# Eight experts' rows: gathers and scatters as indirect DMAs through DRAM, only expert 0 gathered by products, residual and output by token

## The chip, the core and the metric

The kernel runs on one core of one Trainium2 chip. The metric is the device time of one execution in microseconds (us), the median of three runs. All values are float32. The core's engines are TensorE (PE, its weight loads shown as PEld), VectorE (DVE), ScalarE (ACT), GpSimd (POOL) and SyncE (SP), and 16 DMA engines serve its queues. SP's queue carries the loads of weights here.

## The reference

A block of two layers over 256 tokens of width 1024. Layer 0 (a gated linear recurrence, an RWKV-7 mixer, a dense SwiGLU) and the mixer of layer 1 (mLSTM) are not touched by the change. It touches the last part, the mixture of experts, the residual add behind it and the final norm:

```python
def moe_swiglu(xn, w_router, w1, w3, w2):        # xn = rms_norm(x, norm_ffn), 256 x 1024
    logits = (xt @ w_router).astype(jnp.float32)  # 8 experts
    top_logit, top_idx = lax.top_k(logits, TOP_K) # 2 of them per token
    gates = jax.nn.softmax(top_logit, axis=-1)
    ...
    yb = lax.map(expert_block, (buf.reshape(nblk, EXPERT_BLOCK, D), blk_e))  # silu(x @ w1) * (x @ w3) @ w2, hidden 2816
    y_slot = yb.reshape(P, D)[dest] * sorted_g[:, None].astype(xn.dtype)
    out = jnp.zeros((T, D), xn.dtype).at[sorted_tok].add(y_slot)
```

Then `x + moe_swiglu(...)`, and the final RMS norm with its weight `final_norm` gives the output, 256 x 1024.

## The kernel before

Every engine has a program of its own, written by hand; semaphores order them (`wait_ge` on one, `then_inc` on the other). Activations `x` (the residual) and `xn` are kept transposed, 8 tiles of 128 channels x 256 tokens (`KD` = 8). The layers before the experts end near 552 us.

**Routing.** From the router's logits VectorE computes, for each token (128 tokens on the partitions, `CH` = 2 chunks) and each expert, the slot that the token takes among the expert's 96 (`SLOTS`), in `rt[:, 14:16, :]`. If some expert has more than 96 tokens, `flag` is set and the experts run again for further slots (`PASSES`); each engine loads `flag` and branches at the end. With these inputs the second pass isn't run.

**Gather.** `gather_matrices` writes one-hot matrices `OH` (token x slot, scaled by the token's inverse root mean square), and TensorE's `gather` multiplies the tokens, turned to token-major in `xtok`, with them, in three groups of experts, `GATHERS = ((0, 2), (2, 5), (5, 8))`, into PSUM. ScalarE's `gathered` copies the result with the norm's weight to `xg`, 128 channels x 8 x 96 slots for each expert.

**Stages.** `up(n, g)` is half an expert's first two products: for each of 8 weight tiles of 1408 KB (a ring of `USLOTS` = 9 buffers), 24 matmuls of 352 columns, four side by side in the four column groups. ScalarE's `gate` takes the SiLU of it, VectorE's `hidden` multiplies and turns it into `hidT`, 32 x 32 blocks at a time. `down(n, e, p)` takes a pair of second-product weight tiles of 512 KB each (a ring of `DSLOTS` = 7), three turns of four matmuls of 512 columns; eleven pairs make an expert. Its output lies in PSUM banks 6 and 7, where ScalarE's `expert_out` copies it to `ye` (slots on the partitions).

**Scatter.** `scatter_rows` writes `OHg` (one-hot by slot, scaled by the gate; it lies over `hidT`), `scatter_matrices` transposes it on TensorE to `SG`, and `scatter(n, e, r)` multiplies `ye` with it: four matmuls of 256 columns for each half `r` of the channels. VectorE's `add` adds each half to `x`.

**The order around it**, on TensorE, for an expert e: up(2e+2), down pairs 5 to 10 of e, up(2e+3), down pairs 0 to 4 of e+1, with the scatter of e behind pairs 1 and 2. SP's loads follow the same order in `refills`, one load when a buffer is through, waited for in order:

```python
                    refill_up(n, 2 * e + 1)
                    for p in range(5):
                        refill_down(n, NB * e + p)
                    if e < E - 1:
                        refill_up(n, 2 * e + 2)
                    for p in range(5, NB):
                        refill_down(n, NB * e + p)
```

The tile of down pair p that comes free is refilled with the tile 7 further on, three and a half pairs later. Behind the last expert: the branch on `flag`, ScalarE squares `x` (8 tiles of channels), TensorE's `norm_mean` sums over channels, ScalarE's root, VectorE's reciprocal and `normed` write the output's 8 channel tiles, each stored by SP to `out_T`. POOL has no work after 500 us.

## Time and profile before

| | us |
|---|---|
| median of 3 runs | 1334.25 (1334.09 to 1346.22) |
| the profiled execution | 1339.85 |
| its span, first to last instruction | 1338.1 |
| granted TensorE clock, mean | 0.988 |
| HBM read, written | 344.71 MB, 1.05 MB |

A page of the profile gives each engine's busy time and share of the span, the span in 40 slices, the DMA queues, the chain of work that ended last, and groups of like instructions. A float32 matmul call stands in the trace as two matmul records and two weight load records. Four matmuls that run side by side count once in busy time. The name `W` is one large buffer that holds the weight rings (and `ye`, `rt`), `S` one that holds `xg`, `hidT`, `SG` and `OH`, `ps` is PSUM.

### The profile page before, as it was taken

How to read it: one execution, taken by the hardware profiler on the slowest of the kernel's cores; microseconds unless marked ns; L12 is line 12 of the kernel's file. 1: busy time of each engine (PE TensorE's matmuls, PEld its weight loads, DVE VectorE, ACT ScalarE, POOL GpSimd, SP SyncE). 2: the span in 40 equal slices, each digit the busy share in tenths (PEclk: the TensorE clock that was granted, in tenths of full speed). 3: DMA queues.
4: the chain of work that ended last, by engine and by line, in shares of the span. 5: the costliest groups of instructions: out<-in, count | busy, mean ns of one | idle time of the engine just before them, and what ended most of it. 6: DMA issues, size and time to landing. Idle time of an engine off the chain costs nothing.

```text
span 1338.1 us, 26356 instructions
## 1 busy us (share of the span) xinstructions
PE 1284.5 (96%) x12327; PEld 779.4 (58%) x12327; DVE 279.4 (21%) x605; ACT 180.7 (14%) x378; POOL 15.1 (1%) x14
## 2 busy tenths in 40 slices
PE   6999999999999998999999999999999999999995
PEld 5888888888888886754434434434344344344332
DVE  2657462000002734320000001001001000010012
ACT  3415311000001234310101010000000010100002
POOL 0012000000000000000000000000000000000000
PEclk9999999999999998999999999999999999999998
DMA  9500095454007344387899999999999999999551
GB/s 358 206 1 2 25 341 197 148 184 146 1 0 304 116 188 173 154 347 276 318 383 382 351 408 392 353 380 381 387 391 361 376 377 362 405 391 363 193 208 63
DMA packets 72918, 347.56 MB, mean 260 GB/s; under 512 B 5720, under 2 KB 13272, under 8 KB 56160
## 3 DMA queue, kind: packets, MB, share of 16 engines
q1 hardware_dynamic: 72496, 345.68, 66.9%
q8 instruction: 99, 1.62, 0.5%
q10 hardware_dynamic: 304, 0.10, 0.1%
q14 instruction: 19, 0.16, 0.0%
HBM read 344.71 MB, written 1.05 MB: 258 GB/s over the span
## 4 chain that ended last, share of the span: by engine, by line
PE 91%; DMA 4%; DVE 2%; ACT 1%; issue 1%; DVEq 0%; SPq 0%; ACTq 0%
PE ps L480 91%; DMA W<-in_moe 4%; DMA cf<-in_cf 1%; DVE rs L1347 0%; DVE W L1465 0%; DVE xn L1354 0%; ACT S L1231 0%; ACT S L1136 0%; DVE S L1462 0%; DVE W L1464 0%; ACT W L1290 0%; DVE W L1500 0%; DVE W L1498 0%; ACT L1239 0%; ACT L1136 0%
## 5 line engine op out<-in xcount | busy, mean ns | idle before, releaser
L480 PE MATMUL ps<-W,S 128*32 128x352 f32 (+2 forms) x8384 | 701.1, 491 | 13.7 <-DMA W<-in_moe 11.5
L480 PEld LDWEIGHTS ps<-W,S 128*32 128x32 f32 (+1 forms) x8384 | 280.6, 111 | 424.9 <-issue 377.2
L480 PE MATMUL ps<-xn,W 128*128 128x256 f32 (+1 forms) x1456 | 324.4, 383 | 3.2 <-DVE xn L1354 3.0
L480 PEld LDWEIGHTS ps<-xn,W 128*128 128x128 f32 (+1 forms) x1456 | 277.2, 191 | 46.3 <-issue 7.2
L480 PE MATMUL ps<-S,W 128*128 128x256 f32 (+3 forms) x728 | 161.0, 372 | 2.5 <-ACT W L1290 2.5
L1734 DVE TENSOR_TENSOR S<-S,ps 128x352 f32<-128x352 f32 x48 | 25.0, 521 | 589.8 <-ACT S L1282 586.5
L480 PEld LDWEIGHTS ps<-S,W 128*128 128x128 f32 (+3 forms) x728 | 128.5, 186 | 33.2 <-issue 12.8
L1282 ACT ACTIVATE S<-ps 128x352 f32<-128x352 f32 x48 | 20.5, 462 | 544.6 <-PE ps L480 540.9
L480 PE MATMUL ps<-W 64*64 64x64 f32 (+1 forms) x1296 | 50.5, 224 | 3.2 <-DVE W L1500 1.6
L480 PEld LDWEIGHTS ps<-W 64*64 64x64 f32 (+1 forms) x1296 | 46.7, 137 | 7.8 <-issue 4.1
L1562 DVE TENSOR_TENSOR S<-S,ps 128x256 f32<-128x256 f32 x20 | 8.4, 421 | 194.6 <-ACT S L1184 194.6
L1290 ACT ACTIVATE W<-ps 64x512 f32<-64x512 f32 x32 | 18.9, 591 | 143.4 <-PE ps L480 143.1
L1723 DVE TENSOR_TENSOR x<-x,ps 128x1024 f32<-128x1024 f32 x16 | 19.5, 1221 | 69.7 <-PE ps L480 69.7
L1184 ACT ACTIVATE S<-ps 128x256 f32<-128x256 f32 x20 | 7.7, 383 | 195.6 <-PE ps L480 195.6
L1741 DVE STREAM_TRANSPOSE S<-S 128x352 f32<-128x352 f32 x48 | 26.2, 545 | 15.1 <-PE ps L480 11.4
L480 PE MATMUL ps<-xn,cf 128*128 128x256 f32 x32 | 13.4, 607 | 14.5 <-DMA cf<-in_cf 8.8
L480 PE MATMUL ps<-S,xn 128*128 128x288 f32 (+1 forms) x96 | 23.1, 402 | 1.3 <-DVE S L1692 1.0
L480 PEld LDWEIGHTS ps<-S,xn 128*128 128x128 f32 x96 | 18.5, 204 | 5.6 <-issue 1.1
L480 PEld LDWEIGHTS ps<-xn,cf 128*128 128x128 f32 x32 | 10.1, 324 | 17.3 <-DMA cf<-in_cf 8.8
L1060 ACT ACTIVATE S<-x 128x256 f32<-128x256 f32 x24 | 9.0, 416 | 57.4 <-DVE x L1536 57.4
L1536 DVE TENSOR_TENSOR x<-x,ps 128x256 f32<-128x256 f32 x24 | 9.0, 417 | 24.1 <-PE ps L480 24.0
L1354 DVE SCALAR_TENSOR_TENSOR xn<-x,vec,rs 128x256 f32<-128x256 f32 x32 | 13.0, 479 | 0.1
(232 smaller groups left out, 382.8 us busy)
## 6 DMA issues: line engine op xcount, KB each, us to landing
W<-in_moe SPq DMA_DIRECT2D x128, 1408.0 KB, 8.3
W<-in_moe SPq DMA_DIRECT2D x176, 512.0 KB, 6.3
W<-in_l_ffn_w SPq DMA_DIRECT2D x12, 2048.0 KB, 10.4
W<-in_l_w_in SPq DMA_DIRECT2D x5, 2048.0 KB, 21.1
W<-in_l_ffn_w SPq DMA_DIRECT2D x6, 1536.0 KB, 13.6
W<-in_l_w_out SPq DMA_DIRECT2D x2, 4096.0 KB, 20.4
...
```

Source lines behind the costliest of these rows:

```text
L480: return nc.tensor.matmul(o, l, r, start=start, stop=stop, **kw)
L1060: A_(squares[:, k, :], x[:, k, :], ACT.Square).then_inc(sq_done, 1)
L1184: A_(sil0[:, f % 4, :], ps[:, 4 + f % 4, 0:T], ACT.Silu).then_inc(silu_done, 1)
L1282: A_(sil[:, i % 2, :], ps[:, 2 * t, 0:QN], ACT.Silu).then_inc(m_silu, 1)
L1290: ins = A_(ye[64 * b2:64 * b2 + 64, 512 * i:512 * (i + 1)], ps[64 * i:64 * i + 64, 6 + b2, :], ACT.Copy)
L1354: V.scalar_tensor_tensor(dst[:, k, :], x[:, k, :], col(name, k), rs[:, :], ALU.mult, ALU.mult).then_inc(xn_done, 1)
L1536: V.tensor_tensor(x[:, 2 * d + u, :], x[:, 2 * d + u, :], ps[:, d, u * T:(u + 1) * T], ALU.add).then_inc(res_done, 1)
L1562: V.tensor_tensor(hid0[:, f % 4, :], sil0[:, f % 4, :], ps[:, 4 + f % 4, T:2 * T], ALU.mult).then_inc(hid_done, 1)
L1723: V.tensor_tensor(x[:, 4 * r:4 * r + 4, :].rearrange("p d t -> p (d t)"), x[:, 4 * r:4 * r + 4, :].rearrange("p d t -> p (d t)"), ps[:, 2 ...
L1734: V.tensor_tensor(hid, sil[:, i % 2, :], ps[:, 2 * t + 1, 0:QN], ALU.mult).then_inc(m_hid, 1)
L1741: V.transpose(hidT[:, h, t, :], hid).then_inc(m_ht, 1)
```

## The change

- **Gather.** Only expert 0 is still gathered by products (96 columns instead of 192), with `gather(0, 0)`. For the others ScalarE scales the tokens and writes a copy with its channels in another order (`xmv`), POOL stores this to a DRAM buffer `x_rows` (2 DMAs, row 0 is zeros). TensorE multiplies ones with one-hot matrices of the token numbers (`slot_rows`), and VectorE's `slots` makes of it the lists of row numbers `gidx` and `sidx`. POOL's `gather(e)` issues three indirect DMAs of 128 rows x 1 KB for each of experts 1 to 7, into `landed`; VectorE's `gathered` transposes them in 32 x 32 blocks and multiplies by the norm's weight into `xg`. `landed` is one tile, so gather(e) waits for gathered(e - 1).
- **Scatter.** For experts 0 to 6 `expert_out` copies the output to `ye`, and POOL issues two indirect DMAs, 128 rows x 2 KB and 128 rows x 1 KB, to a DRAM buffer `y_rows` (a row for each token and choice, filled with zeros early in the kernel). So that the third turn of a down pair gives whole slots, it is 8 matmuls of 256 columns. Behind expert 6 POOL reads `y_rows` back (4 DMAs of 512 KB) and VectorE adds them by token, with the gates. Expert 7 is still scattered by products, by token (`SG` as weights, `ye` of 512 columns as the other operand).
- **Residual and output by token.** The residual is `xtok`. The final norm works on 128 tokens x 512 channels at a time, with sums of squares by ScalarE's `accum_out`; its weight comes as a row broadcast over the partitions (`wrow`, 512 KB, loaded in the last expert). The output is stored in four pieces.
- **Branch.** `flag` is loaded early, on TensorE between up 0 and the rest; the branch stays at the end of the experts.
- The expert's first weights are laid out for the other order of channels, on the host, with the same sizes.

The core of the diff:

```diff
+            def gather(e):
+                if e > 1:
+                    pool.wait_ge(xg_done, XG0 + e - 1)
+                for b in range(3):
+                    nc.gpsimd.indirect_dma_start(landed[:, T * b:T * (b + 1)], None, x_rows.rearrange("r (i n) -> (r i) n", i=4),
+                                                 bass.IndirectOffsetOnAxis(ap=gidx[:, 3 * e + b:3 * e + b + 1], axis=0)).then_inc(g_in, 16)
+
+            pool.wait_ge(xs_done, XS0 + CH)
+            for c in range(CH):
+                pool.dma_start(x_rows[1 + P * c:1 + P * (c + 1), :], xmv[:, c, :]).then_inc(pool_io, 16)
+            pool.wait_ge(pool_io, 16 * 7)
+            pool.wait_ge(ix_done, IX0 + 1)
+            for e in range(1, 4):
+                gather(e)
+            for e in range(E - 1):
+                pool.wait_ge(m_yout, e + 1)
+                nc.gpsimd.indirect_dma_start(y_rows.rearrange("r (h n) -> (r h) n", h=2), bass.IndirectOffsetOnAxis(ap=sidx[:, 0, e:e + 1], axis=0),
+                                             ye[:, 0:512], None).then_inc(y_sent, 16)
+                nc.gpsimd.indirect_dma_start(y_rows.rearrange("r (h n) -> (r h) n", h=4), bass.IndirectOffsetOnAxis(ap=sidx[:, 1, e:e + 1], axis=0),
+                                             ye[:, 512:768], None).then_inc(y_sent, 16)
+                if e + 4 < E:
+                    gather(e + 4)
+            pool.wait_ge(y_sent, 32 * (E - 1))
+            for a in range(2):
+                for c in range(CH):
+                    pool.dma_start(yback[:, a, c, :], y_rows[1 + T * a + P * c:1 + T * a + P * (c + 1), :]).then_inc(pool_io, 16)
...
+            def slot_rows():
+
+                pe.wait_ge(oh_done, 2)
+                for bank, b0, b1 in ((6, 0, 512), (7, 512, E * SLOTS)):
+                    for c in range(CH):
+                        ins = mm(ps[:, bank, 0:b1 - b0], con(ONES), OH[:, c, :, :].rearrange("p e s -> p (e s)")[:, b0:b1], c == 0, c == 1)
+                ins.then_inc(rr_done, 1)
...
+                    if turn == 2 and n == 0 and e < E - 1:
+                        for u in range(2):
+                            h, b = divmod(2 * p + u, NB)
+                            v = 2 * NB * e + 2 * p + u
+                            for g in range(4):
+                                ins = mm(ps[32 * g:32 * g + 32, 7, 0:T], hidT[:, h, 1, 32 * b:32 * b + 32], w2t[v % DSLOTS][:, T * g:T * (g + 1)],
+                                         p == 0 and u == 0, p == NB - 1 and u == 1, skip_group_check=True)
+                        continue
...
                 act.wait_ge(m_d, NB * (E * n + e + 1))
-                if n or e:
-                    act.wait_ge(m_sc, 2 * (E * n + e))
+                if n == 0 and e:
+                    act.wait_ge(y_sent, 32 * e)
+                if n == 0 and e < E - 1:
+                    A_(ye[:, 0:512], ps[:, 6, :], ACT.Copy)
+                    A_(ye[:, 512:768], ps[:, 7, 0:T], ACT.Copy).then_inc(m_yout, 1)
+                    return
...
+            def gathered(e):
+
+                dve.wait_ge(g_in, 48 * e)
+                step(V.transpose(turned, landed))
+                w0 = VECS["moe_norm"]
+                V.tensor_tensor(xg[:, e, :, :].rearrange("p k (b s) -> p b k s", b=3), turned.rearrange("p (b k s) -> p b k s", b=3, k=KD),
+                                vec[:, w0:w0 + KD].unsqueeze(1).unsqueeze(3).broadcast_to([P, 3, KD, 32]), ALU.mult).then_inc(xg_done, 1)
...
             def experts(n):
                 hidden(n, 0)
+                if n == 0:
+                    slots()
+                    gathered(1)
                 hidden(n, 1)
+                if n == 0:
+                    gathered(2)
                 for e in range(E):
                     if e < E - 1:
                         hidden(n, 2 * e + 2)
                         hidden(n, 2 * e + 3)
-                    for r in range(2):
-                        add(n, e, r)
-
+                        if n == 0 and e + 3 < E:
+                            gathered(e + 3)
```

**The experts' start on TensorE.** The names: `ps<-S,xn` is a gather, `ps<-W,S` with 352 columns an up stage (192 calls), with 512 columns a down turn, `ps<-cf,S` a product of ones or a transpose with constants. Before:

```order
L480 MATMUL ps<-S,xn 128x192 x16
L480 MATMUL ps<-W,S 32x352 x192
L952 MATMUL ps<-cf,S 128x128 x16
L480 MATMUL ps<-S,xn 128x288 x16
L480 MATMUL ps<-W,S 32x352 x192
L480 MATMUL ps<-S,xn 128x288 x16
L480 MATMUL ps<-W,S 32x512 x60
```

With the change, the same stretch of TensorE:

```order
L561 MATMUL ps<-S,xn 128x96 x16
L561 MATMUL ps<-W,S 32x352 x192
L1155 TENSOR_LOAD flag
L1155 ISA x2
L561 MATMUL ps<-S,cf 128x512 x2
L561 MATMUL ps<-S,cf 128x256 x2
L1041 MATMUL ps<-cf,S 128x128 x2
L561 MATMUL ps<-W,S 32x352 x192
L561 MATMUL ps<-W,S 32x512 x8
```

Both later gathers are gone, 14 of 16 transposes too; the load of `flag` and four products have come between the first two up stages.

**An expert on TensorE**, from up(2e+3) over the first down pairs of the next expert. Before, with the two halves of the scatter (`ps<-S,W`) between pairs:

```order
L480 MATMUL ps<-W,S 32x352 x192
L480 MATMUL ps<-W,S 32x512 x24
L480 MATMUL ps<-S,W 128x256 x4
L480 MATMUL ps<-W,S 32x512 x12
L480 MATMUL ps<-S,W 128x256 x4
L480 MATMUL ps<-W,S 32x512 x24
L480 MATMUL ps<-W,S 32x352 x192
```

With the change, two pairs of the same place:

```order
L561 MATMUL ps<-W,S 32x352 x192
L561 MATMUL ps<-W,S 32x512 x8
L561 MATMUL ps<-W,S 32x256 x8
L561 MATMUL ps<-W,S 32x512 x8
L561 MATMUL ps<-W,S 32x256 x8
```

The scatter is gone, and a pair is 8 matmuls of 512 and 8 of 256 columns instead of 12 of 512.

**The end on VectorE.** Before, behind the last adds (x4 for the last two experts), the branch, and the norm by channel:

```order
L1723 TENSOR_TENSOR x<-x,ps 128x1024 x4
L1755 TENSOR_LOAD flag
L1755 ISA x2
L1756 COMPARE_AND_BRANCH
...
L1765 MEMSET misc 128x1
L1347 RECIPROCAL rs<-rs 128x256
L1354 SCALAR_TENSOR_TENSOR xn<-x,vec,rs 128x256 x8
```

With the change, from the four products that add the rows read back (`L1961`) on:

```order
L1961 SCALAR_TENSOR_TENSOR xn<-S,W,xn 128x1024 x4
L1921 COPY W<-ps 64x512 x2
L1973 COMPARE_AND_BRANCH
...
L1916 TENSOR_TENSOR xn<-xn,ps 128x512 x4
L1993 TENSOR_TENSOR misc<-misc 128x1
L1997 RECIPROCAL misc<-misc 128x1
L1989 SCALAR_TENSOR_TENSOR xn<-xn,misc,W 128x512
L1993 TENSOR_TENSOR misc<-misc 128x1
L1989 SCALAR_TENSOR_TENSOR xn<-xn,misc,W 128x512
L1997 RECIPROCAL misc<-misc 128x1
L1989 SCALAR_TENSOR_TENSOR xn<-xn,misc,W 128x512 x2
```

The branch now stands between the copies of the last expert's output and the last adds, and the norm's pieces are 128 x 512 with reciprocals of one column.

## Rows read from the trace of the kernel before

**Rows 1.** Page: busy time of TensorE; GB/s moved in 40 slices of the span.
```profile
PE 1284.5 (96%) x12327; PEld 779.4 (58%) x12327; DVE 279.4 (21%) x605; ACT 180.7 (14%) x378; POOL 15.1 (1%) x14
...
GB/s 358 206 1 2 25 341 197 148 184 146 1 0 304 116 188 173 154 347 276 318 383 382 351 408 392 353 380 381 387 391 361 376 377 362 405 391 363 193 208 63
```

**Rows 2.** Page: the chain that ended last, shares of the span by engine.
```profile
PE 91%; DMA 4%; DVE 2%; ACT 1%; issue 1%; DVEq 0%; SPq 0%; ACTq 0%
```

**Rows 3.** Stretches: us, busy by engine (instructions), PEclk, DMA share, GB/s.
```profile
687.00:1237.00 550.00, 538.47 (x6292) 216.41 (x6288) 53.04 (x84) 29.57 (x60) 0.00 (x0) 1.00 0.97 379
...
1237.00:1311.00 74.00, 74.00 (x788) 27.30 (x780) 8.32 (x13) 3.65 (x7) 0.00 (x0) 1.00 0.54 198
...
688.00:696.00 8.00, 5.27 (x52) 1.37 (x44) 2.13 (x4) 0.00 (x0) 0.00 (x0) 1.00 1.00 412
...
744.00:752.00 8.00, 8.00 (x96) 2.99 (x92) 0.45 (x1) 0.00 (x0) 0.00 (x0) 1.00 0.87 307
```

**Rows 4.** Timeline of the experts' start: start us, us, engine, line, operation, count [idle before].
```profile
558.05 6.89 PE L480 MATMUL ps<-S,xn 128*128 128x192 f32 x32 [0.97 <-DVE S L1692]
...
565.81 28.61 PE L480 MATMUL ps<-W,S 128*32 128x352 f32 x384 [0.87 <-issue]
...
597.78 0.55 DVE L1741 STREAM_TRANSPOSE S<-S 128x352 f32<-128x352 f32 x1 [2.29 <-PE ps L952]
...
605.89 28.61 PE L480 MATMUL ps<-W,S 128*32 128x352 f32 x384
...
634.43 8.18 PE L480 MATMUL ps<-S,xn 128*128 128x288 f32 x32
...
643.20 7.07 PE L480 MATMUL ps<-W,S 128*32 128x512 f32 x64 [0.59 <-ACT S L1267]
```

**Rows 5.** Timeline, TensorE, one expert's two scatter pieces between down pairs.
```profile
736.56 1.99 PE L480 MATMUL ps<-S,W 128*128 128x256 f32 x8
738.49 2.78 PE L480 MATMUL ps<-W,S 128*32 128x512 f32 x24
```

**Rows 6.** Waits from 696 to 1240 us: us in total, times, longest.
```profile
PE ps L480 <- DMA W<-in_moe: 11.5, 6, 2.7
```

**Rows 7.** DMA issues: KB, us to landing; at 0.7, 634, 646, 685, 687, 1008, 734 us.
```profile
x<-in_xT SPq DMA_DIRECT2D x1, 1024.0 KB, 5.9
...
W<-in_moe SPq DMA_DIRECT2D x1, 1408.0 KB, 8.8
...
W<-in_moe SPq DMA_DIRECT2D x1, 512.0 KB, 3.6
...
W<-in_moe SPq DMA_DIRECT2D x1, 1408.0 KB, 9.9
...
W<-in_moe SPq DMA_DIRECT2D x1, 512.0 KB, 8.6
...
W<-in_moe SPq DMA_DIRECT2D x1, 512.0 KB, 8.1
...
W<-in_moe SPq DMA_DIRECT2D x1, 512.0 KB, 6.3
```

**Rows 8.** Timeline of the tail, from the last down matmul on.
```profile
1311.12 2.40 ACT L1290 ACTIVATE W<-ps 64x512 f32<-64x512 f32 x4 [30.95 <-PE ps L480]
...
1313.58 3.72 PE L480 MATMUL ps<-S,W 128*128 128x256 f32 x16 [2.52 <-ACT W L1290]
...
1322.41 0.06 DVE L1765 MEMSET misc<- 128x1 f32 x1 [3.85 <-issue]
...
1322.50 2.56 ACT L1060 ACTIVATE xn<-x 128x256 f32<-128x256 f32 x8 [8.98 <-DVE misc L1765]
...
1330.19 1.75 DVE L1347 RECIPROCAL rs<-rs 128x256 f32<-128x256 f32 x1 [7.72 <-ACT rs L1068]
...
1331.97 3.26 DVE L1354 SCALAR_TENSOR_TENSOR xn<-x,vec,rs 128x256 f32<-128x256 f32 x8
...
1332.49 3.78 SPq L445 DMA_DIRECT2D out_T<-xn  x8
```

More of the change, by code:

```diff
@@ L57 @@
 MEANS, PICK = EYE + L, EYE + L + 32
-NCONST = PICK + 16
+TOK, QUARTER, SIDE, EVEN, ODD, SPARE6, SPARE7 = [PICK + 32 + i for i in (0, 2, 3, 4, 5, 6, 7)]
+NCONST = PICK + 40
+YROWS = 2 * T + 1 + P // 4 + P // 2
 def constants():
@@ L1027, in experts @@
                             down(n, e + 1, p)
-                            if p in (1, 2):
+                            if n and p in (1, 2):
                                 scatter(n, e, p - 1)
@@ L1031, in experts @@
                     scatter(n, E - 1, r)
+            gather(0, 0)
+            up(0, 0)
+            over = pe.value_load(flag[0:1, 0:1], min_val=0, max_val=1)
             experts(0)
-            pe.wait_ge(flag_done, 1)
-            over = pe.value_load(flag[0:1, 0:1], min_val=0, max_val=1)
             with pe.If(over != 0):
                 for n in range(1, PASSES):
-                    pe.wait_ge(m_add, 2 * E * n)
+                    pe.wait_ge(m_add, adds(n, 0))
                     experts(n)
-            norm_mean(4, 4)
         @block.scalar
@@ new lines, in add_half, with last_out @@
+            def add_half(first, c, i, done):
+                dve.wait_ge(m_sc, first + 2 * c + i + 1)
+                return V.tensor_tensor(xtok[:, c, 512 * i:512 * (i + 1)], xtok[:, c, 512 * i:512 * (i + 1)], ps[:, 2 * c + i, :], ALU.add).then_inc(done, 1)
+            def last_out(n):
+                dve.wait_ge(m_d, NB * E * (n + 1))
+                for i in range(2):
+                    V.tensor_copy(ye[64:128, 512 * i:512 * (i + 1)], ps[64 * i:64 * i + 64, 7, :]).then_inc(y_half, 1)
@@ L1753, in _, with added @@
+                last_out(n)
+            def added(n):
+                for c, i in ((0, 0), (0, 1), (1, 0), (1, 1)):
+                    add_half(adds(n, E - 1), c, i, m_add)
+                dve.wait_ge(m_add, adds(n + 1, 0))
+            dve.wait_ge(flag_done, 1)
+            over = dve.value_load(flag[0:1, 0:1], min_val=0, max_val=1)
             experts(0)
-            dve.wait_ge(m_add, 2 * E)
-            over = dve.value_load(flag[0:1, 0:1], min_val=0, max_val=1)
             with dve.If(over != 0):
+                dve.wait_ge(xs_done, XS0 + CH)
@@ new lines, in _, with scaled @@
+                    V.tensor_scalar(rt[:, 14:16, :], rt[:, 14:16, :], -float(SLOTS), None, ALU.add).then_inc(pos_shifted, 1)
+                    dve.wait_ge(pos_shifted, PS0 + turn)
+                    gather_matrices(range(0, 2), False)
+                    gather_matrices(range(2, E), False)
+                    scatter_rows(range(E))
+                    experts(turn)
+                dve.wait_ge(m_sc, adds(PASSES, 0))
+                dve.wait_ge(in_wf, WF0 + 32)
+            def scaled(c, i):
+                o = slice(512 * i, 512 * (i + 1))
+                V.scalar_tensor_tensor(xtok[:, c, o], xtok[:, c, o], frec[:, c:c + 1], wrow[:, o], ALU.mult, ALU.mult).then_inc(xn_done, 1)
@@ new lines, in total, with inverse @@
+            def total(c):
+                dve.wait_ge(sq_done, 4 * KD + 2 * c + 2)
+                V.tensor_tensor(ftot[:, c:c + 1], fsum[:, 2 * c:2 * c + 1], fsum[:, 2 * c + 1:2 * c + 2], ALU.add).then_inc(sum_done, 1)
+            def inverse(c):
+                dve.wait_ge(root_done, 5 + c)
+                step(V.reciprocal(frec[:, c:c + 1], frec[:, c:c + 1]))
+            for c, i in ((0, 0), (0, 1), (1, 0), (1, 1)):
+                add_half(adds(0, E - 1), c, i, xn_done)
+            total(0)
@@ L1769, in inputs_of @@
+            dve.wait_ge(in_wf, WF0 + 16)
+            inverse(0)
+            scaled(0, 0)
+            total(1)
+            scaled(0, 1)
+            inverse(1)
+            scaled(1, 0)
+            scaled(1, 1)
 def inputs_of(i):
```

280 lines of the change are left out of this document (205 added, 75 removed), and 2 rows, old and new, of the table NV.

## The prediction

> **What bounds the kernel now.** I read the page's busy times first: TensorE is busy 96% of the span [rows 1]. The chain that ended last agrees: 91% TensorE, 4% DMA [rows 2]. So time taken off TensorE comes off the end, unless the weight loads take it back. Hence the second view, the stretches [rows 3]. From 687 to 1237 us six experts pass, 550 / 6 = 91.7 us each, with the 16 DMA engines 97% busy at 379 GB/s. The reader is to see that two engines are nearly full at once. In one 8 us piece the queue is behind and runs at 412 GB/s with share 1.00; in another, share 0.87, it has caught up and waits for free buffers.
>
> TensorE's part of an expert's 91.7 us: two up stages at 28.6 us [rows 4]. A stage is 96 fours of matmuls of 352 columns (four column groups side by side), 0.298 us per four, so a four of 512 columns is 0.43. A pair of down tiles is six such fours, 2.6 us, and eleven pairs are 28.6. Together 85.8. The scatter adds two pieces, each 1.93 us to the next matmul (736.56 to 738.49) [rows 5], 3.9 in all. The rest, 1.9, is the wait for weights: 11.5 us in six waits [rows 6].
>
> Where is that wait? A down tile is requested when a pair is through (its slot is free), and is wanted two pairs and a turn later, 2 x 2.6 + 0.85 = 6.0 us. The load issued at 687.3 took 8.6 us [rows 7]; 8.6 - 6.0 is the longest wait, 2.7 [rows 6]. So TensorE waits when a tile takes over 6.0 us to land, which it does after an up stage whose large loads stand ahead of it in SP's queue.
>
> **The change part by part, against the profiled span of 1338.1.**
>
> *Start of the experts.* Removed: gather of expert 1 beside 0 (192 columns become 96), both later gathers, 14 of 16 scatter transposes. The first gather was 32 records of 192 columns in 6.89 us, 0.215 each, the last one 0.256 each with 288 columns; 96 columns are worth 0.04, 1.3 us in 32. ScalarE's copies still end it, so I take 0.8. Its weights are now read at a stride of 8 elements, which no row prices: 0 (the nearest rows, ordinary loads, which lie beside the products) to +6 (as long again as the gather), I take 0. Between up 0 and up 1 there were 605.89 - 594.43 = 11.5 us [rows 4]. Now: a flag load on TensorE's sequencer (VectorE's load and branch took 3.85 us together [rows 8]; I count 1.0 for the load, 2.85 for the branch); four products with ones, two records each, 4 x 0.43 + 4 x 0.21 = 2.6; two transposes, 0.5; then what the gather used to hide: up 1 waits until VectorE has emptied the banks, and its first transpose waits for the scatter transposes (both use one tile). That is two transposes and two products, a transpose being 0.55 [rows 4], 2.3 in all. Sum 6.4, gain 5.1. The last gather, 634.43 to 643.20, 8.8 us, goes entirely. But it let the queue drain: a down tile then took 3.6 us. Without it the first down tile stands behind up loads of 8.8 us [rows 7]; tiles land about 1.3 sooner than the up load before them (9.9 and 8.6 around 687), 7.5 - 6.0 = 1.5 us of wait. Start: 0.8 + 5.1 + 8.8 - 1.5 = **13 us**.
>
> The new chain beside it: ScalarE's four scalings (up to 1.1 us each by the halves in [rows 8]) lie under up 0. The row numbers are ready on VectorE about 8 us after up 0 ends; then three row gathers, a transpose of 768 columns and a product (1.2 + 0.9 by the 352-column rows). VectorE has these ahead of emptying up 1, due 28.6 us after up 1 starts. Some 14 us are left; beyond that each us is TensorE's.
>
> *Six loaded experts.* Scatter gone: -3.9. The third turn of a pair has 8 matmuls of 256 columns instead of 4 of 512: the same columns; the weight loads that double in it lie beside matmuls (PEld is busy 216 of 550 us [rows 3]), 0. The scatter pauses however gave the queue time: the first tile ahead of each pause took 6.3 to 8.1 us (six of them: 6.3, 7.6, 7.5, 8.1, 7.2, 6.3; [rows 7] has the least and the largest). Less 6.0 these become new waits, 7.1 us in six, 1.2 each. That alone leaves 85.8 + 1.9 + 1.2 = 88.9. Added traffic: 3 gathers of 128 x 1 KB (four experts of this stretch), a scatter of 128 x 2 KB and 128 x 1 KB: 0.79 MB. At 412 GB/s 1.9 us of all engines; by the load of x, 1 MB of 1 KB rows in 5.9 us [rows 7], 4.6. The queue's own sum: 16 x 1408 KB + 22 x 512 KB = 34.6 MB at 379 / 0.97 = 391 GB/s is 88.5 us, and 2.0 for the rows: **90.5**. The larger sum decides, 90.5 for 91.7: 1.2 x 6 = **7 us**. Most of the removed TensorE time turns into waits on weights.
>
> The Trainium skill ("DMA: Bandwidth & Descriptors", Specifications) gives an HBM limit of about 358 GB/s per core. By it an expert's 35.4 MB would take 99 us and the change would cost 7 us per expert. With 13 + 4 + 13 outside them, the end would be 1334 - 30 + 42 = 1346. The rows do not bear that out (379 GB/s over 550 us), so it gets no chance of its own.
>
> *Last expert.* No up loads stand ahead; from 1237 us on TensorE never waits and the DMA share is 0.54 [rows 3]. The seventh scatter goes whole: **4 us**. The 2 MB read back and the 512 KB norm row fall into up 15, when the queue is idle; if not, 2.6 us per MB.
>
> *Tail.* Before, 1311.1 to 1338.1, 27.0 us: four copies 2.4, products 3.7, add, branch to 1322.4, squares with mean 7.3, root, a reciprocal of 256 columns 1.75, eight products 3.3, stores 2.9 [rows 8]. After: the copies split over two engines, products from +0.7 to +4; VectorE's copies and then its branch of 2.85 hold the first add to +4.1; four adds of 0.6 to +6.6; square, root and reciprocal of a single column for the second tokens to +9; two products of 0.65 to +10.3; store of 256 KB 3.2: 13.5 to 14. Gain **13 us**.
>
> *Elsewhere.* The zero fill (2 MB) falls where the queue moves 1 to 25 GB/s [rows 1]: 0. If it came late it would hold SP's FFN loads.
>
> Sum: 13 + 7 + 4 + 13 = 37, span 1301. The profiled execution took 1339.85, 5.6 over the median of the runs, so I count from the median: 1334 - 37 = 1297.
>
> **The rivals.**
> *Row transfers hide (chance 0.20).* The piece at 412 GB/s speaks for it: 35.4 MB at 412 are 86 us, about TensorE's own 85.8. Then the landings seen set the cycle, 88.9: 2.8 x 6 = 17 instead of 7. About 1287. Against: six of six first tiles are over 6.0 already.
> *Small rows cost more than their bytes (0.17).* 4.6 us an expert instead of 2.0 gives 93.1, 1.4 x 6 = 8 lost: 13 - 8 + 4 + 13 = 22, about 1312. A slow start chain or strided weight read gives the same.
> *The rows sit on one engine (0.08), slower.* A load counts only when all 16 engines are through. If a row DMA's 128 rows go to one engine, each row at 0.06 to 0.09 us (1024 rows on 16 engines in 3.9 to 5.9), a DMA lasts 8 to 12 us there, 16 to 60 per expert: about 1334 - 30 + 6 x 35 = 1510. It decides from 47 / 6 = 7.8 us per expert on, 47 being the sum without any row cost, waits included. Nothing in the profile is an indirect DMA, so only the even spread of the ordinary loads speaks against.
> *No gain to be measured (0.05):* gathers land after up 1 and on the path of several experts, +25: about 1323.
> By the Trainium skill (same page, Queues, rings and completion order) an engine takes turns between queue rows by packet. By this POOL's rows would not queue behind SP's loads, but each tile would land later by the rows' time; no row shows it yet.
>
> **How the numbers follow.** Likeliest (0.50): 1297, on its own 1290 to 1308 (2.0 a cycle either way would be 12, some of it excluded by the two sums). 1283 to 1324 takes in both neighbours and the no-gain case, leaving the one-engine case out. 1% is 13 us, about what a measurement of this kernel tells from nothing. Faster takes the first three less a part of the third: 0.84; same 0.08; slower 0.08.
>
> **What would show it.** Right: no gap of the weight stream between 600 and 643 us; first down matmul about 628 to 631; 90 to 91 us per expert with DMA share near 1.0; waits on in_moe risen from 11.5 to 25 to 35 us; last matmul to end 13 to 15 us; clock as before. Wrong: an expert under 89 or over 92.5 us, a TensorE wait on xg or hidden near 600 to 640, or a POOL chain longer than an up stage.

## The result, and the profile after

| | before | after |
|---|---|---|
| median, us | 1338.74 (4 runs, 1334.09 to 1346.22) | 1303.21 (4 runs, 1297.44 to 1304.02) |
| the profiled execution, us | 1339.85 | 1297.44 |
| its span, us | 1338.1 | 1295.6 |
| granted TensorE clock, mean | 0.988 | 0.985 |

The ratio is 0.9715 (95% interval 0.9667 to 0.9762), beside the forecast 1297 / 1334.25 = 0.972. By the medians the total came out as forecast; the terms behind it did not.

The page of the kernel after: busy time of the engines, the queue that GpSimd issues, and the chain that ended last. They answer to [rows 1] and [rows 2].

```profile
PE 1239.5 (96%) x12737; PEld 760.6 (59%) x12737; DVE 281.3 (22%) x618; ACT 164.7 (13%) x347; POOL 56.1 (4%) x61
...
q0 software_dynamic: 3376, 10.75, 2.1%
...
PE 87%; DMA 9%; DVE 2%; ACT 1%; issue 1%; DVEq 0%; SPq 0%
```

TensorE's busy time fell by 45 us (1284.5 to 1239.5), the span by 42.5. The chain lost 4% in TensorE and gained 5% in DMA: part of the work that left came back as waits. The 42.5 is more than the 35.5 between the medians: the execution profiled before lies 1.1 us over the median before, the one after is the fastest of its four, 5.8 us under the median after. The table of parts below rests on these two executions.

Stretches of the kernel after; columns: us, busy time by engine (instructions), granted clock, DMA share, GB/s. 680.08 to 1212.95 are the six loaded experts, as 687 to 1237 in [rows 3].

```profile
680.00:1213.00 533.00, 514.80 (x6727) 215.75 (x6720) 47.48 (x82) 20.63 (x48) 23.44 (x24) 1.00 1.00 399
1213.00:1284.00 71.00, 69.87 (x808) 25.70 (x800) 11.23 (x16) 2.74 (x6) 4.15 (x6) 1.00 0.67 247
```

A cycle (one expert of the steady state) is 532.9 / 6 = 88.8 us for 91.7. TensorE computes 514.8 / 6 = 85.8 of it, as forecast, and the bytes now pass at 399 GB/s. The prediction had 391 GB/s from before and let it decide (90.5). Its waits in the same stretch (us in total, times, longest), for [rows 6]:

```profile
PE ps L561 <- DMA W<-in_moe: 18.2, 17, 1.9
```

18.2 us in 17 waits: 3.0 a cycle for 1.9. The Trainium skill ("DMA: Bandwidth & Descriptors", Specifications) gives a limit of about 358 GB/s of HBM per core; the trace disagrees, 399 GB/s over 533 us with one core at work. The same page (Bandwidth) calls that figure the share of a core when both cores of the HBM domain stream, so it was not the one for this kernel.

The start of the experts on TensorE (start us, us, engine, line, operation, count, idle before), for [rows 4]:

```profile
558.48 7.92 PE L561 MATMUL ps<-S,xn 128*128 128x96 f32 x32 [0.49 <-DVE S L1832]
567.12 30.98 PE L561 MATMUL ps<-W,S 128*32 128x352 f32 x384 [0.71 <-issue]
598.02 2.85 PE L561 MATMUL ps<-S,cf 128*128 128x512 f32 x8
...
603.62 37.20 PE L561 MATMUL ps<-W,S 128*32 128x352 f32 x488 [2.54 <-DVE S L1931]
642.84 43.20 PE L561 MATMUL ps<-W,S 128*32 128x512 f32 x544 [2.01 <-DMA W<-in_moe]
```

The new chain on GpSimd and VectorE in that time:

```profile
609.38 1.03 POOL L535 DMA_INDIRECT S<-x_rows,gidx  x1 [33.28 <-DVE gidx L1898]
...
612.01 0.95 POOL L535 DMA_INDIRECT S<-x_rows,gidx  x1 [0.30 <-issue]
...
618.20 0.98 DVE L1903 STREAM_TRANSPOSE S<-S 128x768 f32<-128x768 f32 x1 [9.65 <-DMA S<-x_rows,gidx]
...
619.21 0.96 DVE L1905 TENSOR_TENSOR S<-S,vec 128x768 f32<-128x768 f32 x1
```

An indirect DMA of 128 rows keeps GpSimd for 1.0 us, and the three pieces for expert 1 are in the buffer 5.2 us after the last is issued (612.96 to 618.20). VectorE is back at 620.2, and its next work is due at 632.8: 12.6 us to spare, where the prediction had some 14. None of it is on the path.

The tail, for [rows 8]:

```profile
1283.42 1.21 ACT L1416 ACTIVATE W<-ps 64x512 f32<-64x512 f32 x2 [26.95 <-PE ps L561]
1283.49 1.41 DVE L1921 COPY W<-ps 64x512 f32<-64x512 f32 x2 [19.65 <-PE ps L561]
...
1284.32 3.67 PE L561 MATMUL ps<-W,S 128*128 128x512 f32 x8 [0.97 <-DVE W L1921]
...
1286.33 1.28 ACT L1451 ACT_TABLE_LOAD   x1 [1.70 <-issue]
1286.39 2.48 DVE L1916 TENSOR_TENSOR xn<-xn,ps 128x512 f32<-128x512 f32 x4 [1.50 <-PE ps L561]
...
1291.74 1.42 DVE L1989 SCALAR_TENSOR_TENSOR xn<-xn,misc,W 128x512 f32<-128x512 f32 x2
```

From the last down product to the end are 12.2 us (1283.4 to 1295.6) for 27.0.

Where the 42.5 us of the profiled spans went:

| part | before | after | gained | forecast |
|---|---|---|---|---|
| ahead of the experts | to 550.8 | to 551.7 | -0.9 | 0 |
| start, to the first loads of the steady state | 136.6 (to 687.3) | 128.4 (to 680.1) | 8.2 | 13 |
| six loaded experts | 550.1 | 532.9 | 17.2 | 7 |
| last expert | 73.7 | 70.4 | 3.3 | 4 |
| tail | 27.0 | 12.2 | 14.8 | 13 |

Two terms are off by more than 2 us: the start gave 5 less than forecast, the cycles 10 more. The experiments ask why. A caution on single executions: the gather of expert 0 starts anywhere from 558.1 to 563.7 us in the profiles below, for reasons in the earlier layers that no run here looks into, so I compare stretches inside the experts, and whole times by their ratios.

### The profile page after: what moved, and what is told of

It is laid out like the page before. It is cut to its first block, busy times and chain, and to the rows that moved or that the text cites. A ratio compares the mean times of both kernels' runs of the same rounds, so it can differ in the third digit from the quotient of the medians.

```text
span 1295.6 us, 27195 instructions
## 1 busy us (share of the span) xinstructions
PE 1239.5 (96%) x12737; PEld 760.6 (59%) x12737; DVE 281.3 (22%) x618; ACT 164.7 (13%) x347; POOL 56.1 (4%) x61
## 4 chain that ended last, share of the span: by engine, by line
PE 87%; DMA 9%; DVE 2%; ACT 1%; issue 1%; DVEq 0%; SPq 0%
PE ps L561 87%; DMA W<-in_moe 8%; DMA cf<-in_cf 1%; DVE W L1604 0%; ACT S L1351 0%; ACT S L1256 0%; DVE S L1601 0%; DVE W L1603 0%; DVE xn L1989 0%; ACT S L1454 0%; DVE rs L1486 0%; DVE W L1639 0%; ACT L1451 0%; ACT L1359 0%; ACT L1256 0%
## 5 line engine op out<-in xcount | busy, mean ns | idle before, releaser
L561 PE MATMUL ps<-W,S 128*32 128x352 f32 (+3 forms) x9008 | 707.7, 470 | 25.6 <-DMA W<-in_moe 20.7
L561 PEld LDWEIGHTS ps<-W,S 128*32 128x32 f32 (+1 forms) x9008 | 301.1, 111 | 430.9 <-issue 347.5
L561 PE MATMUL ps<-S,W 128*128 128x256 f32 (+3 forms) x600 | 130.0, 370 | 0.0
L561 PEld LDWEIGHTS ps<-S,W 128*128 128x128 f32 (+3 forms) x600 | 106.0, 187 | 15.5 <-issue 1.1
L1938 DVE STREAM_TRANSPOSE S<-S 128x352 f32<-128x352 f32 x48 | 26.2, 545 | 14.8 <-PE ps L561 11.4
L535 POOL DMA_INDIRECT S<-x_rows,gidx x21 | 20.2, 960 | 183.9 <-DVE S L1905 146.4
L547 POOL DMA_INDIRECT y_rows<-W,idx x7 | 6.9, 991 | 433.8 <-ACT W L1410 433.8
L1409 ACT ACTIVATE W<-ps 128x512 f32<-128x512 f32 x7 | 4.2, 597 | 109.1 <-PE ps L561 109.1
L561 PE MATMUL ps<-S,cf 128*128 128x512 f32 (+2 forms) x40 | 13.1, 518 | 0.8 <-ACT S L1288 0.8
L561 PE MATMUL ps<-xn,cf 128*128 128x256 f32 x16 | 5.4, 511 | 8.7 <-DMA cf<-in_cf 8.7
L1278 ACT ACTIVATE W<-ps 128x512 f32<-128x512 f32 (+1 forms) x20 | 11.1, 555 | 15.8 <-PE ps L561 15.6
```

The source lines that it names most:

```text
L535: nc.gpsimd.indirect_dma_start(landed[:, T * b:T * (b + 1)], None, x_rows.rearrange("r (i n) -> (r i) n", i=4), bass.IndirectOffsetOnAxis( ...
L547: nc.gpsimd.indirect_dma_start(y_rows.rearrange("r (h n) -> (r h) n", h=2), bass.IndirectOffsetOnAxis(ap=sidx[:, 0, e:e + 1], axis=0), ye[ ...
L561: return nc.tensor.matmul(o, l, r, start=start, stop=stop, **kw)
L1278: A_(XX[:, q, 0:w].rearrange("p x j t -> p (x j t)"), ps[:, 4 + q, 0:w * T], ACT.Copy).then_inc(xcp, 1)
L1409: A_(ye[:, 0:512], ps[:, 6, :], ACT.Copy)
L1938: V.transpose(hidT[:, h, t, :], hid).then_inc(m_ht, 1)
```

## The experiments

**Theory.** In the steady state TensorE's own work (85.3 to 85.8 us) and the lateness of the down tiles set the cycle. A down tile is requested 6.0 us ahead of its use because there are seven slots for them; what lands later is a wait. The row transfers are nearly free in it. **Rival.** The transfers are full (DMA share 1.00): bytes at about 400 GB/s set 88.8, and each byte of rows costs. For the start, a second question: what made the gather and the first up stage slower than forecast.

### The changed kernel again

> The changed kernel once more, as the base for the runs beside it. Both theories: 1297 to 1304 us, cycle of a loaded expert 88.8 us, the first product stage of expert 0 in about 29 to 31 us. If the granted clock of 0.92 in that stage came from the change, it shows again; if it was of that execution, the stage takes 28.6 as before.

Measured: median 1301.22 us, ratio to before 0.9748 (0.9702 to 0.9793), six cycles in 532.7 us, up 0 again 31.00 us. So the longer stage belongs to the change.

### Without the scatters, and with three times as many

e1_no_scatter leaves the two row DMAs out:

```diff
@@ GpSimd, for e in range(E - 1)
-                nc.gpsimd.indirect_dma_start(y_rows..., ye[:, 0:512], None).then_inc(y_sent, 16)
-                nc.gpsimd.indirect_dma_start(y_rows..., ye[:, 512:768], None).then_inc(y_sent, 16)
@@ ScalarE
-                    act.wait_ge(y_sent, 32 * e)
```

> The changed kernel without the scatters of experts 0 to 6: their two indirect transfers and the wait for them are left out, so the buffer holds zeros. Each expert moves 128 x 3 KB = 0.39 MB less. If transfer bandwidth sets the cycle (399 GB/s, share 1.00), a cycle shortens by 1.0 us and the kernel by 6 to 7 us. If the cycle is TensorE's work of 85.8 us plus what the down tiles land later than 6.0 us after their request, and the row transfers are hidden, it shortens by 0 to 0.4 us and the kernel by 0 to 2.5.

e2_scatter_x3 issues them for three buffers:

```diff
-                nc.gpsimd.indirect_dma_start(y_rows..., ye[:, 0:512], None).then_inc(y_sent, 16)
...
+                for yr in (y_rows, y_rows2, y_rows3):
+                    nc.gpsimd.indirect_dma_start(yr..., ye[:, 0:512], None).then_inc(y_sent, 16)
...
-                    act.wait_ge(y_sent, 32 * e)
+                    act.wait_ge(y_sent, 96 * e)
```

> The changed kernel with each scatter of experts 0 to 6 issued three times, two of them into buffers that nobody reads: 0.79 MB more for each expert and 4 more indirect issues on GpSimd (about 4 us of it). If bandwidth sets the cycle, it grows by 2.0 us and the kernel by 12 to 14 us. If latency of the down tiles does, 0 to 1.0 us for each cycle, 0 to 6 in all. If small rows or their issue on GpSimd cost more than their bytes, over 14.

Measured: without scatters 1299.38 us, ratio 0.9713 (0.9679 to 0.9748), six cycles 533.8 us, a cycle 89.0. With three 1308.80 us, ratio 0.9781 (0.9736 to 0.9827), six cycles 546.2, a cycle 91.0. Taking 0.39 MB away gives nothing; adding 0.79 MB costs 2.2 us. The first is as my theory expected, the second is what the rival did (2.0); I had 0 to 1.0. The 2.2 is read from one execution each; the medians lie only 7.6 us apart (1308.80 for 1301.22), less than the rival's 12 to 14, with over 11 us between the slowest and the fastest execution of either kernel. Waits of the kernel without scatters, then of the one with three:

```profile
PE ps L556 <- DMA W<-in_moe: 19.2, 16, 2.3
```

```profile
PE ps L562 <- DMA W<-in_moe: 25.1, 16, 3.2
```

Of the 13.3 us more than after the change, 6.9 are waits (25.1 for 18.2). The other 6.4 are in TensorE's own work (521.1 for 514.7), and the stretches of the three-scatter kernel show how. A 2.0 us wait ends at 825.15:

```profile
822.00:825.00 3.00, 1.14 (x16) 0.14 (x7) 0.00 (x0) 0.00 (x0) 1.91 (x2) 1.00 1.02 408
825.00:827.00 2.00, 1.84 (x16) 0.70 (x20) 0.00 (x0) 0.00 (x0) 0.00 (x0) 0.65 1.00 397
827.00:829.00 2.00, 2.00 (x20) 0.75 (x16) 0.00 (x0) 0.00 (x0) 0.00 (x0) 0.50 1.03 420
829.00:831.00 2.00, 2.00 (x32) 0.83 (x28) 0.00 (x0) 0.00 (x0) 0.00 (x0) 1.00 1.06 397
```

Behind the wait the granted clock is 0.50, the lower of the two levels (1.2 GHz for 2.4), until about 829. In four of the six cycles TensorE was busy 87.2 to 87.6 us for 85.8 and the granted clock was 0.98, 1.4 to 1.8 us for each: these four waits (2.0 to 3.2 us) were paid for twice. Not every long wait was: behind one of 2.86 us at 735 the clock stayed at 1.00. Waits alone would have been 1.1 a cycle.

The kernel before has one such stretch too, which the prediction's sum left out. Behind a 2.6 us wait the same 496 records take 42.3 us, where they take 40.6 in four of the other five cycles (the fifth 40.7); the second line is a stretch of it:

```profile
1061.94 42.32 PE L480 MATMUL ps<-W,S 128*32 128x512 f32 x496 [2.62 <-DMA W<-in_moe]
```

```profile
1064.00:1066.00 2.00, 2.00 (x12) 0.43 (x8) 0.00 (x0) 0.00 (x0) 0.00 (x0) 0.50 0.61 221
```

### Another split of the same buffer: 8 up slots, 9 down slots

```diff
-USLOTS = 9
-DSLOTS = 7
+USLOTS = 8
+DSLOTS = 9
...
+        in_d = (in_d + [in_qkv, in_xm, in_z, in_wo1])[0:DSLOTS]
...
-            load_u(0, 8)
...
-                        sp.wait_ge(m_u, UNITS - KD)
+                        sp.wait_ge(m_u, UNITS)
                         sp.dma_start(wrow, A["wf"].broadcast_to([P, D])).then_inc(in_wf, 16)
```

The load of the final norm's row also moves behind the first down loads of the last expert.

> The changed kernel with 8 slots for up units and 9 for down tiles in place of 9 and 7; nothing is left out, bytes are the same. A down tile is then requested one pair of tiles (2.8 us) earlier, 8.8 us ahead of its use. Latency theory: the 18 us of TensorE waits on down tiles in the six cycles fall under 4, the cycle to 85.8 to 86.5 us, the kernel by 13 to 18 us. Bandwidth theory: cycle 88.8 as now, no change over 2 us, the waits only move to other tiles.

Measured: 1273.19 us (1271.63 to 1275.08), ratio 0.9519 (0.9494 to 0.9545), 28 us under the changed kernel measured beside it (1301.22). Its waits and a stretch of the steady state:

```profile
PE ps L561 <- DMA W<-in_moe: 1.4, 3, 0.6
```

```profile
690.00:1200.00 510.00, 508.64 (x6688) 217.35 (x6684) 47.49 (x82) 20.36 (x48) 23.45 (x24) 1.00 1.01 415
```

The same bytes pass at 415 GB/s, six cycles take 513.1 us, 85.5 each, and the waits are 1.4 us in all. This decides between the two theories: 399 GB/s at share 1.00 was not the limit of the transfers. (Nor need 415 be: TensorE hardly waits here, so this is the rate that it asked for.) The edit also takes an up slot away, so fewer large loads might have stood ahead of the down tiles. The landings speak against that: a down tile took 8.7 us from issue to landing (median of the page) for 7.2 after the change, later and not sooner, and was in time because it was requested 8.8 us ahead. The share stood at 1.00 to 1.01 at both rates, so it doesn't tell how near the limit is. It gave more than I expected (13 to 18). By the profiles 19.8 come from the six cycles (16.8 in waits, 3.0 in TensorE's own work), and another 3.8 from the first wait in the start and the low clock behind it, which are gone too (34.0 us of 34 busy at clock 1.00 from 640 to 674). That is 23.6 of the 24.3 us between the two profiled spans; the medians lie 28.0 apart.

e4_ring_7_11 has 7 and 11 (same edits with these numbers, `for i in (4, 5, 6)`).

> The changed kernel with 7 up slots and 11 down slots. With 8 and 9 the waits on weights fell to 1.4 us in all, so latency theory leaves nothing to gain: within 2 us of the 8 and 9 kernel (1273). If the up units now come late (seven slots of 3.6 us each are 25 us ahead), waits appear in the up stages, 3 us or more over it. Either way it stays 20 us or more under the changed kernel.

Measured: 1275.12 us, ratio 0.9530 (0.9496 to 0.9565), six cycles 511.8 us, waits 0.5 us in all. As expected nothing more is to be had from slots: 85.3 a cycle is TensorE's own work.

### Rows on the deeper ring

e9_ring_scatter_x3 has both edits, three scatters and 8 and 9 slots.

> The kernel with each scatter issued three times (two into buffers that nobody reads), now with 8 up slots and 9 down slots. With 9 and 7 the two further scatters cost 2.2 us in each cycle, 7 us in waits on down tiles and 6 us in TensorE work at the lower clock behind the longest of them. If they cost through the lateness of the down tiles, the deeper ring hides most of it: cycle 85.5 to 87.0 us, where 36.2 MB at the 416 GB/s seen with this ring are 87.0. If each scatter costs its 1.1 us whatever the ring, the cycle is 87.5 to 88 and the kernel 13 us over the 8 and 9 kernel.

```profile
PE ps L562 <- DMA W<-in_moe: 10.4, 7, 1.9
```

```profile
690.00:1200.00 510.00, 499.64 (x6564) 212.56 (x6560) 44.81 (x77) 20.63 (x48) 46.75 (x48) 1.00 1.01 415
```

Measured: 1285.25 us, ratio 0.9632 (0.9596 to 0.9668), six cycles 523.1 us, 87.2 each: 0.2 over the first range, near the 87.0 by bytes, and under the 87.5 to 88 of the other case. TensorE waits again here, 10.4 us. The rate is 415 GB/s with and without the extra rows, so with this ring the transfers look to be at their limit, and further rows cost about their bytes: 1.7 us a cycle for 0.79 MB. The whole kernel however lies 12 us over the 8 and 9 kernel (measured at another time), close to the 13 that I had tied to the other case; the cycles say 10.0 of it.

### The kernel before with the same two edits

b1_before_ring_8_9 has the slots of 8 and 9. b2_before_no_scatter leaves the scatter products and their additions of experts 0 to 6 out, with the waits between them adjusted (not shown):

```diff
             def scatter(n, e, r):
+                if n == 0 and e < E - 1:
+                    return
...
                 if n == 0 and e < E - 1:
+                    return
                 dve.wait_ge(m_sc, ...)
```

> The kernel before, with 8 slots for up units and 9 for down tiles. Latency theory: its 11.5 us of TensorE waits on weights nearly vanish, 8 to 12 us faster (ratio 0.991 to 0.994), cycle 91.7 to about 89.8 us, which is TensorE's own work with scatters. Bandwidth theory: within 2 us of before.

> The kernel before with the scatter products of experts 0 to 6 and their additions left out, and nothing in their place: no row transfers, no indirect DMA. The landing times of before gave 88.9 us for a cycle without them; after the change it measures 88.8 with 0.79 MB of rows in it. If rows are hidden, the cycle here is 88.5 to 89.2. If rows cost their bytes at 400 GB/s, it is 86.5 to 87.3, and the change lost 2 us in each cycle to them.

Measured: with the slots 1324.38 us, ratio 0.9901 (0.9858 to 0.9944), no wait on weights is left, and a cycle is 89.2 us (535.5 / 6), which is 85.3 and the scatter's 3.9. Without scatters 1319.82 us, ratio 0.9860 (0.9820 to 0.9900), six cycles 531.5 us, 88.6 each, with these waits (stretch of the steady state):

```profile
PE ps L480 <- DMA W<-in_moe: 16.5, 12, 2.2
```

That is 0.2 us under the changed kernel's 88.8. One of its waits (2.0 us at 965) has the low clock behind it, 45.75 us for 44.06 in the cycle before, 1.7 us; without that a cycle is 88.3, 0.5 under. So the landing arithmetic of the prediction (88.9) was close, and the rows cost 0.2 to 0.5 us a cycle in place, not 2.0. They are 0.66 MB a cycle on average, 0.79 in the four that have a gather.

### The gather of expert 0: stride or width

e5_contiguous reads the weights without the stride, e7_wide keeps it and doubles the columns:

```diff
@@ e5_contiguous
-                        rows = (xsc if n else xtok)[:, c, :].rearrange("p (m k) -> p k m", k=KD)[:, k, :]
+                        rows = ... if n else xtok[:, c, k * P:(k + 1) * P]
@@ e7_wide
-                                 OH[:, c, e0:e1, :].rearrange("p e s -> p (e s)"), c == 0, c == 1)
+                                 OH[:, c, 0:1, :].broadcast_to([P, 2, SLOTS]) ..., c == 0, c == 1)
```

> The changed kernel whose gather of expert 0 reads its weights as 128 contiguous columns in place of every eighth; expert 0's features then stand in another order than its weights, so its part of the output means something else. After the change the gather took 7.9 us and ran at a granted clock of 0.50, which lasted 13 us, into the first up stage (31.0 us against 28.6). If the stride is the cause: gather 4 to 5.5 us, low clock 3 to 4 us as before, up 0 28.6 us, the kernel 3 to 5 us faster than the changed one. If the narrower products (96 columns instead of 192) are: gather and clock as after the change, the time within 1 us of it.

> The changed kernel whose gather of expert 0 computes each product over 192 columns (its 96 twice), half of which nobody reads; the weights keep the stride. If the narrow products cause the long low clock: low clock 3 to 4 us, gather 6 to 7 us, up 0 28.6 us, the kernel 1 to 3 us faster than the changed one. If the stride does: gather 8 to 10 us, the low clock stays 13 us or more, no gain.

The granted clock (third column from the end) in three stretches from 557 to 571.5 us in the kernel before, after, contiguous and wide, in this order:

```profile
557.00:561.00 4.00, 3.03 (x10) 2.96 (x10) 3.93 (x19) 0.23 (x1) 0.00 (x0) 0.57 1.02 419
561.00:566.00 5.00, 4.13 (x28) 3.83 (x31) 0.54 (x4) 3.20 (x9) 0.00 (x0) 1.00 0.81 324
566.00:571.50 5.50, 5.50 (x80) 2.90 (x76) 3.99 (x18) 2.50 (x3) 0.00 (x0) 1.00 0.19 36
```

```profile
557.00:561.00 4.00, 3.51 (x20) 3.42 (x20) 2.23 (x13) 1.41 (x5) 0.00 (x0) 0.66 1.01 411
561.00:566.00 5.00, 5.00 (x23) 5.00 (x22) 0.00 (x0) 1.45 (x6) 0.00 (x0) 0.50 0.94 381
566.00:571.50 5.50, 4.79 (x34) 1.97 (x37) 2.69 (x13) 5.03 (x6) 0.00 (x0) 0.50 0.02 9
```

```profile
557.00:561.00 4.00, 3.51 (x25) 3.42 (x25) 2.18 (x13) 1.60 (x5) 0.00 (x0) 0.81 1.02 414
561.00:566.00 5.00, 4.29 (x40) 3.46 (x43) 0.11 (x1) 3.28 (x9) 0.00 (x0) 0.81 0.91 370
566.00:571.50 5.50, 5.50 (x82) 2.87 (x74) 5.32 (x25) 5.50 (x4) 0.00 (x0) 1.00 0.47 141
```

```profile
557.00:561.00 4.00, 2.67 (x19) 2.34 (x17) 3.13 (x22) 1.35 (x4) 0.00 (x0) 0.90 0.98 399
561.00:566.00 5.00, 5.00 (x21) 5.00 (x19) 0.67 (x4) 1.15 (x4) 0.00 (x0) 0.74 1.03 419
566.00:571.50 5.50, 4.79 (x40) 3.74 (x43) 0.26 (x2) 3.03 (x7) 0.00 (x0) 1.00 0.28 111
```

And the gather and the stage behind it, contiguous, then wide:

```profile
558.22 5.44 PE L561 MATMUL ps<-S,xn 128*128 128x96 f32 x32 [0.49 <-DVE S L1832]
564.37 28.61 PE L561 MATMUL ps<-W,S 128*32 128x352 f32 x384 [0.71 <-issue]
```

```profile
560.29 8.68 PE L561 MATMUL ps<-S,xn 128*128 128x192 f32 x32 [0.49 <-DVE S L1837]
569.68 28.61 PE L561 MATMUL ps<-W,S 128*32 128x352 f32 x384 [0.71 <-issue]
```

A stretch of 4.0 us at 0.57 holds 4.0 x (1 - 0.57) x 2 = 3.4 us at the lower level (0.50). So counted, the low clock lasts 3.4 us before, 3.4 contiguous, 3.4 wide, and 13.2 after the change, through the whole gather and some 5 us of up 0. It does so in all eight profiles with strided weights and 96 columns: from 556 to 580 us each has a mean granted clock of 0.72, a gather of 7.92 to 7.96 us and an up 0 of 30.98 to 31.12. Contiguous, the gather takes 5.44; wide, 8.68; up 0 is 28.61 in both. So in these single profiles undoing either of the two, stride or width, went with a short low clock, and my expectation for the wide one was half wrong: clock and up 0 as for "the narrow products", the gather as for "the stride". The stride has a price of its own, seen at equal width and 3.4 us of low clock each: 8.68 for the 6.89 of [rows 4] (6.98 and 7.04 in the other two kernels with contiguous weights of 192 columns).

The times: contiguous 1296.91 us, ratio 0.9716 (0.9668 to 0.9764), 0.003 under the changed kernel's second measurement (0.9748) and level with its first (0.9715), so the 3 to 5 us expected can't be told; wide 1304.08 us, 0.9770 (0.9722 to 0.9818). In the contiguous profile the first wait on a down tile grew from 2.0 to 3.9 us: of the 4.9 us that gather and up 0 gain, 1.9 come back as this wait at seven slots, and more as the low clock behind it.

### Without the second pass

e6_one_pass leaves out the flag's loads and the branches:

```diff
-            over = pe.value_load(flag[0:1, 0:1], min_val=0, max_val=1)
             experts(0)
-            with pe.If(over != 0):
...
```

> The changed kernel without the code of the second pass: the loads of the flag on four engines and the branches on it are left out (with this input the branch is not taken, the arithmetic is the same). The prediction priced the load on TensorE at 1.0 us at the start and the branch at 2.85 us in the tail. After the change the chain shows 0.7 us at the start and 1.7 us in the tail as issue. If those are the load and the branch, 2 to 3 us faster than the changed kernel; if something else fills them, within 1 us.

```profile
1289.58 1.28 ACT L1427 ACT_TABLE_LOAD   x1
...
1290.38 0.69 DVE L1892 TENSOR_TENSOR xn<-xn,ps 128x512 f32<-128x512 f32 x1 [0.55 <-PE ps L547]
```

Measured: 1302.31 us, ratio 0.9741 (0.9697 to 0.9785), no difference. The 1.7 us ahead of ScalarE's table load are gone (1289.58 follows the copy at once), and VectorE's first add waits 0.55 us for TensorE's product where it stood idle for 1.50. The next adds wait for the products in turn, so the tail only falls to 11.4 us for 12.2. The 0.71 us at the start is still there: it is not the load. The prediction's 1.0 and 2.85 on the path were 0 and at most 0.8.

### Both edits together

e8_ring_contiguous has 8 and 9 slots and the contiguous gather, made right by laying out expert 0's weights in that order:

```diff
+    w13[0] = np.stack([a(name)[0].reshape(KD, P, 4, 2, QN).transpose(3, 0, 1, 2, 4) for name in ("l1_moe_w1", "l1_moe_w3")], 3)
...
-  A_(xg[:, e0:e1, k, :], ..., ACT.Copy, scale=col("moe_norm", k))
+  A_(xg[:, 0, k, :], src[:, 0:SLOTS], ACT.Copy, scale=col("l1_norm_ffn", k))
```

> The changed kernel with 8 up slots and 9 down slots, and the gather of expert 0 with contiguous weights; expert 0's norm column and the rows of its two up matrices (arranged when the weights are laid out) follow the order that this gives, so nothing is left out. If both effects add: 1273 from the ring alone, less 4 to 5 from the gather and the low clock behind it, 1267 to 1270 us (ratio 0.948 to 0.951). If the transfers bound the start once the wait on down tiles is gone, the gather's gain comes back as a wait on weights and it stays at 1271 to 1274.

```profile
558.83 7.06 PE L561 MATMUL ps<-S,xn 128*128 128x96 f32 x32 [0.49 <-DVE S L1844]
566.59 28.61 PE L561 MATMUL ps<-W,S 128*32 128x352 f32 x384 [0.71 <-issue]
...
600.73 40.02 PE L561 MATMUL ps<-W,S 128*32 128x352 f32 x520 [2.54 <-DVE S L1943]
641.25 9.03 PE L561 MATMUL ps<-W,S 128*32 128x512 f32 x120 [0.50 <-DMA W<-in_moe]
```

Measured: 1271.22 us median of 6 (1269.59 to 1279.20), ratio 0.9524 (0.9493 to 0.9555). 66 us under before and some 30 under the changed kernel. Beside the ring alone (0.9519) no gain can be told. The time fell in my second range (1271 to 1274), but not for its reason: the waits on weights are 0.8 us in all, so no gain came back as a wait. In this profile the low clock covered the whole gather (7.06 us, not 5.44) though the weights are contiguous, and ended with it, so up 0 took 28.61: 2.5 us less than with the stride. How long the clock stays low is thus not settled by stride and width alone.

## Why the prediction was right, and where its working was not

**Total.** 37 us were forecast, 35.5 separate the medians, 42.5 the two profiled spans. The 7.0 us between the last two are the 1.1 and 5.8 by which the two profiled executions lie off the medians; in which stretch a typical execution has them no profile shows. The forecast counted from the median of three runs because the profile before was 5.6 us over it; with more runs the medians of before were 1334.7 to 1338.7, so up to 4 over that of the first three, and those of after 1301.2 and 1303.2. So the total is right to within some 4 us, not better, and the agreement within 2 is luck: the terms, read from the profiles, sum to 5.5 more than forecast.

**Six loaded experts, 7 forecast, 17.2 found: the failing step is "The larger sum decides, 90.5".** That sum divided the bytes by 391 GB/s, a rate measured while the queue was held up by full slots; 415 GB/s flow with nine down slots (e3_ring_8_9), and 35.4 MB at that rate are 85.3. (The 415 is that cycle's own rate, so this shows that 391 was no limit, and not where the limit is.) By the prediction's own sign, "an expert under 89", the term was wrong: 88.8. The other sum, made from landings, said 88.9 and was close twice: 88.6 without rows (b2_before_no_scatter), 88.8 with them. The first rival, that row transfers hide, describes what the steady state did. "2.0 for the rows" was 0.2 to 0.5 in place. One part of it was right by two errors: TensorE's own work without waits is 85.3 (e4_ring_7_11) and not 85.8; the kernel before had 0.3 a cycle of low clock that the sum left out, and some 0.2 us of extra busy time go with each wait (514.7 us with 17 waits, 511.7 with 3). That rows cost nothing at any amount is not true: three times the scatters cost 2.2 us a cycle. "Waits risen to 25 to 35" was 18.2 (20.7 with the start).

**The start, 13 forecast, 8.2 found.** Four steps, by the rows above and [rows 4]:
- The first gather: 0.8 gain forecast. From its start to that of up 0 it takes 8.64 us for 7.76, 0.9 lost: low clock and stride, taken as 0 with an end of +6.
- Up 0: 0 forecast, 2.4 lost (30.98 for 28.61), all of it the granted clock. "Clock as before" failed here.
- Between the up stages 6.4 forecast, 5.5 found, a gain of 5.9 for 5.1; the flag load costs nothing. Its last part, the wait for VectorE, is 2.54 us, where the sum had 2.3.
- The last gather gone, 8.8, as forecast; the first down tile waited 2.0 for 1.5. Behind that wait the clock fell once more, another 1.8 us in the work up to 680. The stretches of the kernel after show it:

```profile
642.00:644.00 2.00, 1.16 (x12) 0.49 (x16) 0.00 (x0) 0.00 (x0) 0.00 (x0) 0.91 1.03 412
644.00:646.00 2.00, 2.00 (x24) 0.89 (x18) 0.00 (x0) 0.00 (x0) 0.00 (x0) 0.50 1.02 408
646.00:648.00 2.00, 2.00 (x18) 0.49 (x13) 0.00 (x0) 0.00 (x0) 0.00 (x0) 0.74 1.03 408
648.00:650.00 2.00, 2.00 (x36) 1.03 (x32) 0.00 (x0) 0.00 (x0) 0.00 (x0) 1.00 1.02 404
```

Together -0.9 - 2.4 + 5.9 + 8.8 - 2.0 - 1.8 = 7.6, and 0.5 came in the routing ahead of the gather: 8.1 for the measured 8.2.

**Last expert**, 4 forecast, 3.3 found: the scatter's 3.9 are gone, and a wait of 0.5 us stands at its start.

**Tail**, 13 forecast, 14.8 found. The first add came at +3.0 and not at +4.1: it stood idle for 1.50 us with the branch and for 0.55 without it (e6_one_pass), so the branch holds it for 0.95 us and not 2.85. The end lay 2.4 us behind the last product of VectorE (1293.16), where 3.2 were taken for the store.

**The rivals.** No row DMA sat on one engine: median landing 6.1 us for a gather's, 5.8 for a scatter's on the page, under a full queue, where 8 to 12 was the case that would have cost. The prediction also cited the rule that an engine takes turns between queues, by which down tiles land later by the rows' time. The page's median landing of a 512 KB tile was 6.3 us before, 6.7 without scatter products and without rows (b2_before_no_scatter), 7.1 with the gathers alone, 7.2 after the change, 7.4 with three times the scatters. From the second to the fourth the cycle is nearly the same (88.6 and 88.8) and rows are what the change adds to the transfers, so about half of the 0.9 us of lateness goes with the rows and half with TensorE's faster pace. By the rule that the prediction cited (the Trainium skill, "DMA: Bandwidth & Descriptors", Queues, rings and completion order: an engine takes turns between the queue rows by packet) each tile would land later by the rows' share; the trace agrees in kind, 0.5 us, and no run tells how the turns were taken.

The two large misses had opposite signs (-4.8 and +10.2) and cancelled in part; the rest, 5.5 us, is hidden by the choice of executions. Right total, two wrong terms.
